# Two attentions: probabilities scaled before they are transposed, and the values matmul turned round

## What is computed

```
def masked_softmax(s, mask):
    s = jnp.where(mask, s.astype(jnp.float32), NEG)
    pr = jax.nn.softmax(s, axis=-1)
    return jnp.where(mask, pr, 0.0)
...
    gt = jax.nn.sigmoid(gates.astype(jnp.float32)).reshape(B, T, 3, NSA_HEADS, 1)
    out = (gt[:, :, 0] * to_bthd(o_cmp) + gt[:, :, 1] * to_bthd(o_sel)
           + gt[:, :, 2] * to_bthd(o_win))
```

```
        p = masked_softmax_2(jnp.concatenate([s_sel, s_own], axis=-1),
                           jnp.concatenate([m_sel, m_own], axis=-1)).astype(v.dtype)
...
        return (jnp.einsum('hqnk,hqnkd->hqd', p_sel, v_sel)
                + jnp.einsum('hqk,hqkd->hqd', p_own, v_own))
...
    mixed = jax.nn.sigmoid(ga) * (o_a @ w_proj_a) + jax.nn.sigmoid(gb) * (o_b @ w_proj_b)
```

## Time and profile before

| | before |
|---|---|
| median of 3 runs | 1384.17 us (1383.19 to 1384.9) |
| profiled execution | 1385.43 us, its span 1383.6 us |
| TensorE busy | 1177.2 us, 85% of the span |
| VectorE, ScalarE, GpSimd busy | 471.0, 255.0, 144.9 us |
| mean granted clock | 0.936 of full speed |
| read from memory | 328.64 MB |
| chain that ended last | DMA 22%, TensorE 16%, ScalarE 3%, VectorE 2% of the span |

### The profile page before, as it was taken

One profiled execution on the slowest core, in us unless ns is written; L12 is line 12 of the kernel. 1 busy time (PEld: TensorE's weight loads), 2 busy tenths in 40 slices (PEclk: granted clock), 3 DMA queues, 4 the chain that ended last, 5 costly groups with the idle time before them and its releaser, 6 DMA issues. The chain is left out here.

```text
span 1383.6 us, 14289 instructions
## 1 busy us (share of the span) xinstructions
PE 1177.2 (85%) x6103; PEld 672.5 (49%) x6103; DVE 471.0 (34%) x771; ACT 255.0 (18%) x502; POOL 144.9 (10%) x159
## 2 busy tenths in 40 slices
PE   7999999999999999999999999997656375564636
PEld 7946655555865999444544446453212031221312
DVE  7672333024715554644784452231001010010101
ACT  2331003125611212001222265011000000000001
POOL 1111004010110124431032000100000000000000
PEclk9999999999999999999999999999788787887879
DMA  9641223352115544344353210898999999999994
GB/s 385 243 182 62 90 95 120 112 211 103 62 37 207 191 183 164 140 182 165 140 196 135 81 59 31 359 412 336 427 429 427 428 427 429 428 429 428 428 423 175
DMA packets 27701, 330.68 MB, mean 239 GB/s; under 512 B 4192, under 2 KB 4976, under 8 KB 7408
## 3 DMA queue, kind: packets, MB, share of 16 engines
q1 hardware_dynamic: 27632, 329.70, 59.1%
HBM read 328.64 MB, written 1.05 MB: 238 GB/s over the span
## 5 line engine op out<-in xcount | busy, mean ns | idle before, releaser
L228 PE MATMUL ps<-ring,arena 128*128 128x512 f32 (+2 forms) x1880 | 685.5, 620 | 88.2 <-DMA ring<-in_w 49.1
L228 PE MATMUL ps<-arena 128*128 128x128 f32 (+9 forms) x2706 | 512.2, 420 | 78.5 <-DMA ring<-in_w 22.1
L228 PEld LDWEIGHTS ps<-ring,arena 128*128 128x128 f32 (+2 forms) x1880 | 261.1, 164 | 402.6 <-issue 396.8
L228 PEld LDWEIGHTS ps<-arena 128*128 128x128 f32 (+3 forms) x2706 | 290.2, 171 | 227.5 <-issue 190.7
L1944 DVE TENSOR_TENSOR arena<-ps,junk 128x512 f32<-128x512 f32 x8 | 5.5, 692 | 366.7 <-PE ps L228 366.7
L228 PE MATMUL ps<-misc,arena 128*32 128x512 f32 (+3 forms) x216 | 83.1, 546 | 23.2 <-DMA arena<-in_w 23.2
L228 PE MATMUL ps<-arena,ring 128*128 128x128 f32 x768 | 88.1, 275 | 0.0
L228 PEld LDWEIGHTS ps<-arena,ring 128*128 128x128 f32 x768 | 87.0, 192 | 0.5 <-issue 0.5
L231 PE MATMUL ps<-cst,arena 128*128 128x128 f32 x456 | 60.0, 275 | 5.2 <-ACT arena L474 2.1
L231 PEld LDWEIGHTS ps<-cst,arena 128*128 128x128 f32 x456 | 51.4, 141 | 26.6 <-issue 16.3
L367 DVE TENSOR_TENSOR arena<-ring 128x2048 f32<-128x2048 f32 (+1 forms) x19 | 36.8, 1937 | 40.4 <-PE ps L228 39.5
(11 more groups left out here) (275 smaller groups left out, 642.1 us busy)
## 6 DMA issues: line engine op xcount, KB each, us to landing
arena<-in_w SPq DMA_DIRECT2D x42, 2048.0 KB, 35.0
ring<-in_w SPq DMA_DIRECT2D x42, 2048.0 KB, 34.2
ring<-in_w_in SPq DMA_DIRECT2D x27, 2048.0 KB, 7.9
ring<-in_w_up SPq DMA_DIRECT2D x8, 2048.0 KB, 8.3
ring<-in_w_down SPq DMA_DIRECT2D x8, 2048.0 KB, 7.8
misc<-in_w SPq DMA_DIRECT2D x8, 2048.0 KB, 34.7
ring<-in_w_out SPq DMA_DIRECT2D x4, 2048.0 KB, 14.6
ring<-in_w_branch_a SPq DMA_DIRECT2D x2, 2048.0 KB, 10.1
```

The costliest lines, as they stand in the source:

```text
L228: return lambda q: q.matmul(out_, l, r, start=s, stop=e, skip_group_check=skip)
```

## The change

The reciprocal of the row sums (times the gate, in the first attention) is taken in a new step `normed`, and GpSimd multiplies the exponentials by it before they are transposed. `pipeline` writes it behind `soft` of the next job. In `values` the roles are exchanged: the values of a head (128 keys x 64) are stationary, the transposed probabilities move, and heads with even and odd place write to PSUM partitions 0-63 and 64-127, two column tiles. In the first attention two heads that share their values go through one matmul (`per_v` is 2), 256 columns; in the second each head has its own, 128 columns. The outputs come out with features on partitions. So in the first block the compressed branch is transposed into `YBT` ahead of the pipeline and each job adds its output there; in the second each job copies into `OT`. The transposes behind are gone, and in the second attention the copy of the transposed probabilities moves from ScalarE to VectorE.

```diff
+        def attention(m, heads, q_of, k_of, v_of, per_v, mask, PT, coef_of, finish, *tokens):
...
+            def normed():
+                t = dve.op(lambda q: q.reciprocal(cc, su), state["e"])
+                gate = coef_of(m, heads)
+                if gate is not None:
+                    t = dve.op(lambda q: q.tensor_tensor(cc, cc, gate, ALU.mult), t)
+                aux[("g", r3_)] = state["e"] = pool.op(lambda q: q.tensor_tensor(S3, S3, cc.unsqueeze(2).broadcast_to([128, H, nk]), ALU.mult), t)
+
             def turned():
...
-                t = act.op(lambda q: q.activation(PT[b], P[:, :], ACT.Copy), t, aux.get(("p", b)))
+                if coef_of(m, heads) is None:
+                    t = dve.op(lambda q: q.tensor_copy(PT[b], P[:, :]), t, aux.get(("p", b)))
+                else:
+                    t = act.op(lambda q: q.activation(PT[b], P[:, :], ACT.Copy), t, aux.get(("p", b)))
...
             def values():
                 P, i = unit()
+                pt = PT[b].rearrange("p (a k q) -> p a k q", a=H, k=m + 1)
                 fns = []
-                for a, h in enumerate(heads):
+                for a0 in range(0, H, 2 * per_v):
                     for kt in range(m + 1):
-                        x = (a * (m + 1) + kt) * 128
-                        fns.append(mm(P[:, a * 64:a * 64 + 64], PT[b][:, x:x + 128], v_of(h, kt), kt == 0, kt == m))
+                        for r in range(2):
+                            o = P[64 * r:64 * r + 64, a0 * 64:(a0 + 2 * per_v) * 64]
+                            fns.append(mm(o, v_of(heads[a0 + r], kt), pt[:, a0 + r:a0 + 2 * per_v:2, kt, :], kt == 0, kt == m))
...
@@ pipeline
                 if x < n:
                     jobs[x][3]()
+                if 1 <= x < n + 1:
+                    jobs[x - 1][4]()
                 if x % every == 0:
                     fill(1)
...
+        ybt = [turn_half(OBN, YBT, None, m, cmp_t[m], qt_toks) for m in range(2)]
+
+        def fin_nsa(m, heads, P, t):
+            c = heads[0] // 2
+            o = YBT[:, c:c + len(heads) // 2, m * 128:m * 128 + 128]
+            ybt[m] = dve.op(lambda q: q.tensor_tensor(o, P, o, ALU.add), t, ybt[m])
+            return ybt[m]
...
-        pipeline(jobs, 2, lambda: ybt.append(turn_half(OBN, YBT, None, 0, ob_tok[0], qt_toks)))
+        pipeline(jobs, 2)
...
-                a = dve.op(lambda q: q.tensor_tensor(OO[w][:, m, heads[0]:heads[0] + H], P[:, 0:H * 64].rearrange("p (h d) -> p h d", h=H),
-                                                     cc.unsqueeze(2).broadcast_to([128, H, 64]), ALU.mult), a)
...
+                a = dve.op(lambda q: q.tensor_copy(o, P), t)
...
-        pipeline(jobs, 1, lambda: turn_out(0))
+        pipeline(jobs, 1)
...
-        proj_a.pop(0)()
-        turn_out(1)
-        t_ot = [pe.now(), act.now()]
+        t_ot = [pe.now(), act.now(), dve.now(), pool.now()]
```

More of the change, by code:

```diff
@@ L1004, in build @@
         sm = sb("sm", 32)
+        cn4 = sb("cn4", 32)
         aux = {"s": 0}
-        def attention(m, heads, q_of, k_of, v_of, mask, PT, finish, *tokens):
+        def attention(m, heads, q_of, k_of, v_of, per_v, mask, PT, coef_of, finish, *tokens):
             H, nk = len(heads), 128 * (m + 1)
@@ L1013, in attention @@
             nm, su = nmx[:, r3_ * 8:r3_ * 8 + H], sm[:, r3_ * 8:r3_ * 8 + H]
+            cc = cn4[:, r3_ * 8:r3_ * 8 + H]
             state = {}
@@ L1051, in values @@
                 P, i = unit()
+                pt = PT[b].rearrange("p (a k q) -> p a k q", a=H, k=m + 1)
                 fns = []
-                for a, h in enumerate(heads):
+                for a0 in range(0, H, 2 * per_v):
                     for kt in range(m + 1):
-                        x = (a * (m + 1) + kt) * 128
-                        fns.append(mm(P[:, a * 64:a * 64 + 64], PT[b][:, x:x + 128], v_of(h, kt), kt == 0, kt == m))
+                        for r in range(2):
+                            o = P[64 * r:64 * r + 64, a0 * 64:(a0 + 2 * per_v) * 64]
+                            fns.append(mm(o, v_of(heads[a0 + r], kt), pt[:, a0 + r:a0 + 2 * per_v:2, kt, :], kt == 0, kt == m))
                 t = pe.group(fns, state["p"], unit_users[i])
                 aux[("p", b)] = t
-                unit_users[i] = aux[("g", r3_)] = finish(m, heads, P, su, t)
-            return scores, turned, values, soft
+                unit_users[i] = finish(m, heads, P[:, 0:H * 64].rearrange("p (c q) -> p c q", q=128), t)
+            return scores, turned, values, soft, normed
         def pipeline(jobs, every, late=None):
@@ L1140, in build, with gate_of @@
         tap("ocmp", U(11), cmp_t)
[L1142 to L1157, removed]
+        YBT = U(3).rearrange("p (c t) -> p c t", c=8)
+        OBN = U(11).rearrange("p (m n) -> p m n", m=2)
+        ybt = [turn_half(OBN, YBT, None, m, cmp_t[m], qt_toks) for m in range(2)]
[4 more added lines that the diff above has]
+            return ybt[m]
+        def gate_of(branch):
+            return lambda m, heads: gt3[:, m, branch * 16 + heads[0]:branch * 16 + heads[0] + len(heads)]
         def qr_of(h, m):
@@ L1170, in build @@
                         lambda h, nk, KTT=KTT: KTT[64 * (h % 2):64 * (h % 2) + 64, h // 4, 0:nk],
[L1171 to L1175, removed]
+                        lambda h, kt, voff=voff: KV[:, kt, voff + (h // 4) * 64:voff + (h // 4) * 64 + 64], 2,
+                        cmask[:, 128:256] if m == 0 else cmask[:, 0:256], PT1, gate_of(br), fin_nsa,
+                        qrt_toks, qt_toks, kd[kn], t_cm, kv_toks, cmp_t, t_gt))
         MTT = U(4).rearrange("p (c t) -> p c t", c=8)
@@ L1180, in build @@
         PTT = U(13)[:, 1024:1536].rearrange("p (c t) -> p c t", c=2)
[L1181 to L1183 removed]
+        mtt, t_v, t_h1, t_h2, t_u = [], [], [], [], []
+        pipeline(jobs, 2)
         while fillers:
@@ L1197, in build @@
         weigh_by_half(lambda i: A["w_branch_b"][i], YBT, 8, ybt, GB, gb_t, GA, mg_t,
-                      {(0, 0): lambda: ybt.append(turn_half(OBN, YBT, None, 1, ob_tok[1], qt_toks)), (0, 1): None, (1, 0): None,
+                      {(0, 0): None, (0, 1): None, (1, 0): None,
                        (1, 1): lambda: mtt.append(turn_half(GA, MTT, None, 0, mg_t[0]))})
@@ L1582, in build, with f @@
         SS[2] = U(12, 0.5)
-        OO = [U(6, 0.5).rearrange("p (m h d) -> p m h d", m=2, h=8), U(6, 0.5, 1024).rearrange("p (m h d) -> p m h d", m=2, h=8)]
+        OT = [U(7, 0.5).rearrange("p (c t) -> p c t", c=4), U(7, 0.5, 1024).rearrange("p (c t) -> p c t", c=4)]
         PT2 = [U(13, 0.5), U(13, 0.5, 1024)]
-        fin_toks = [[], []]
+        ot = [[], []]
         def fin2(w):
[L1589 to L1592, removed]
-                a = dve.op(lambda q: q.tensor_tensor(OO[w][:, m, heads[0]:heads[0] + H], P[:, 0:H * 64].rearrange("p (h d) -> p h d", h=H),
-                                                     cc.unsqueeze(2).broadcast_to([128, H, 64]), ALU.mult), a)
-                fin_toks[w].append(a)
+            def f(m, heads, P, t):
+                c = heads[0] // 2
+                o = OT[w][:, c:c + len(heads) // 2, m * 128:m * 128 + 128]
+                a = dve.op(lambda q: q.tensor_copy(o, P), t)
+                ot[w].append(a)
                 return a
@@ L1610, in build @@
                         lambda h, nk, kT=kT: kT[64 * (h % 2):64 * (h % 2) + 64, h // 2, 0:nk],
[L1611 to L1625, removed]
-        pipeline(jobs, 1, lambda: turn_out(0))
-        tap("o2", U(6), fin_toks)
+                        lambda h, kt, vv=vv: vv[:, kt, h * 64:h * 64 + 64], 1,
+                        mask, PT2, lambda m, heads: None, fin2(w), tT[qn], tT[kn], tV[vn], t_dm if w else t_cm, pe.now()))
+        pipeline(jobs, 1)
         fill(8)
```

## The result

The changed kernel takes **1392.02 us** (median of 5 runs, 1391.46 to 1392.9) against 1384.17 us: ratio 1.0053, 95% interval 1.0042 to 1.0065, so slower. Its profiled execution took 1391.66 us, span 1389.9 us; that of before 1385.43, span 1383.6.

What follows compares the result with a forecast made beforehand. TensorE's own sequence was taken to bound the kernel up to about 932 us. First attention +10.6 and second -2.0 gave +8.6 us, so a median of 1392.8, range 1387 to 1403.

Steps and rivals of the forecast that it cites:

- first scores to the projection behind transposes(0): Start of the first attention: the first transposes wait 5.64 us less one scores group, +4.6 us.
- three pairs with a projection: First attention, projections in every second iteration: 14.67 us, then 15.74 twice, from one to the next; +1.9, +1.2, +1.2.
- three iterations without one: First attention, three iterations without a projection: 13.07 us instead of 11.46, +1.6.
- tail: End of the first attention, from transposes(9) on: 9.8 us instead of 9.69, +0.1.
- second attention with its transposes: Second attention: shorter values and absent output transposes save 6.1 us, waits at start and end cost 4.1; -2.0 us.
- Values at 1.07: Both attentions: a values group in two column tiles takes 1.07 us instead of 1.82, bounds 0.86 and 1.82.
- rival 2: Column tiles give nothing and values stay at 1.82 us: +7.1, 1399.9 us; chance 0.08.
- The handoff of 5.64: From the end of the next job's scores to a job's transposes: 5.64 us, 2.37 of it the GpSimd multiply.
- The clock: First attention stage: if new gaps bring the granted clock to the lower level, the time lies above the forecast; no size.
- Weights: Behind the second attention: early expert weights issued some 5 us sooner, counted as nothing.
- Rival 1: TensorE's work alone decides, scaled tiles always ready in both attentions: 1368.2 us; chance 0.08 for any gain.
- Rival 3: GpSimd is held up beside VectorE, +1.31 us in 8.5 places: +11.1, 1403.9 us; chance 0.10.

Runs made afterwards that it cites:

- on_vector: The changed kernel with the multiply by the reciprocals on VectorE instead of GpSimd: 1388.99 us, ratio 1.003 to the kernel before.
- second_only: Only the second attention is changed, the first stays as in the kernel before: 1382.12 us, ratio 0.9987.
- no_scaling: The changed kernel without reciprocal, gate and GpSimd multiply, so its output is wrong and only the attentions are read: 1412.33 us, not comparable.
- one_deeper: The changed kernel with one more pipeline iteration between scores and transposes: 1377.17 us, ratio 0.9948 to the kernel before.
- deeper_apart: The changed kernel with one more pipeline iteration and the first attention's projections in iterations 2, 5, 8 and 11: 1369.76 us, ratio 0.9899 to before.
- first_only: Only the first attention is changed, the second stays as in the kernel before: 1394.1 us, ratio 1.0075.
- tiles_apart: The changed kernel issuing all values matmuls of one column tile, then all of the other: 1392.41 us, ratio 1.0074 to the kernel before.
- multiply_twice: The changed kernel with a second GpSimd multiply, by ones, ahead of the scaling one: 1418.63 us, ratio 1.026 to the kernel before.

## Why the prediction came out right, and where its steps were off

It forecast 1392.8 and the reason: slower, because the scaled tiles come late. Part by part, from the rows above:

| step | forecast | measured |
|---|---|---|
| transposes ahead of the pipeline | +0.9 | +0.9 |
| first scores to the projection behind transposes(0) | +4.6 | +4.6 (15.61 for 11.04), 0.4 of it clock |
| three pairs with a projection | +1.9, +1.2, +1.2 | +2.4 (1.25 clock), +0.4, +0.6 |
| three iterations without one | +1.6 | +0.95 |
| tail | +0.1 | -0.5 |
| group of transposes gone behind | -0.9 | -0.8 |
| second attention with its transposes | -2.0 | -1.8, 1.0 of clock in it |
| sum | +8.6 | +6.7 |

(The spans of the two traced executions differ by 6.3 us, and the one of the changed kernel is 0.6 us ahead at 310 us: 6.9 in all, 0.2 of it behind the second attention. The medians differ by 7.9.)

1. **What bounds it**: held. From the projection behind the second attention on, the rest is 521.4 us against 522.0 - 0.9 (the old output transposes), so the shift reaches the end.
2. **Values at 1.07**: held (1.07 and 1.08), and rival 2, no gain from column tiles, is out. The Trainium skill's page TensorEngine Tiling (Array Packing), section Key Properties, says that different tiles can load and multiply in parallel; the trace agrees, 1.08 with two tiles against 1.94 with one.
3. **The handoff of 5.64**: the place was right, the size was not. The multiply took 1.90, the lower bound, not the 2.37 that I took from the line through 256 and 512 elements, and the handoffs a little less than 0.1 each: 4.99 in all. In some 7 places that is 4.6 us too much. With a multiply of 1.90 the prediction's own sum, over its 8.5 places, would have been 8.6 - 4.0 = 4.6 and its median 1388.8, 3.2 us below the measured one. The page GPSIMD Engine Reference of the Trainium skill (section Elementwise — side-by-side cycle accounting), whose rate of about 2.6 cycles an element gave 2.2 us as an estimate, was nearer than my line, and still above the 1.90 measured.
4. **The clock**: named as what would make it wrong, but not in the sum. Against the same work elsewhere, 1.7 us behind the first wait (transposes 1.36 to the next start for 0.92, projection 8.22 for 6.97) and 1.0 at the end of the second attention (865.08 to 868.54, 3.46, where on_vector at full clock has 2.42, from 865.04 to 867.46). So 2.7 us of the 6.7 are clock, and they hid more than half of the error of point 3. The nearness of 1392.8 to 1392.02 is partly luck. on_vector's rows:

```profile
865.04 1.09 PE L228 MATMUL ps<-arena 128*64 128x128 f32 x16
866.43 1.09 PE L228 MATMUL ps<-arena 128*64 128x128 f32 x16 [0.29 <-DVE arena L1058]
```

5. **Second attention**: turn(0) came 0.1 later, not 0.7; the wait near the end was 2.35, not 3.05, both mostly by the shorter multiply (0.47 of 0.6 and of 0.7). That it gains at all is confirmed by second_only barely (interval to 0.9999), and there not by the stage in the trace.
6. **Weights**: issued some 2.4 us behind the start of the last values instead of 7.5, and worth nothing, as counted (without the old transposes the rest grew by 0.2).
7. **Rival 1**, TensorE's work alone: needs the chain hidden. no_scaling and one_deeper show that it does come then, but not in full: ScalarE's exponentials and copies leave 3.0 us of waits in either. With the projections apart as well, deeper_apart takes 1369.76 us, 1.6 above the 1368.2 of that rival. **Rival 3**, GpSimd held up, is out: 1892 to 1897 ns.

What is shown: the scaling costs 13.8 us in the first attention, against a gain of 5.4 for the rest of the change there, and 12.2 us go away when the transposes stand one iteration further off. What is only argued: the split of the measured +6.7 into multiply and clock, which rests on one trace. first_only has the same first attention and took 3.3 us longer in it, though its waits for GpSimd are less (14.0 us against 15.1), so the clock's part differs by some 4 us from one execution to another.

## What to carry to other kernels

A step added between two engines costs its whole length only where the pipeline has no work beside it: compare the sum of the chain, with what stands ahead of each link in its engine's queue, with the other engine's work in that time. If it is longer, lengthen the distance or put large work into the gap before touching the step; here one iteration and another place for four projections turned +8 us into -14, with the same instructions. And a wait on TensorE costs more than itself if the clock falls behind it.

## What the runs showed of the hardware

- The granted clock fell to the 1.2 GHz level behind short stops of TensorE, and not each time behind the same one. first_only, at the very place where after kept 1.00 (transposes in 1.09 us at 359.48 behind 1.77 us):

```profile
355.26 1.97 PE L231 MATMUL ps<-cst,arena 128*128 128x128 f32 x8 [1.77 <-POOL arena L1050]
```

```profile
356.00:358.00 2.00, 2.00 (x8) 1.48 (x7) 0.33 (x3) 0.73 (x1) 1.56 (x1) 0.50 0.00 0
```

- It also falls with TensorE busy throughout, in some executions only. The same stretch ahead of the change, behind 32 records of 48 columns (16 matmuls), in before, with the window 250 to 300 us:

```profile
251.30 3.67 PE L228 MATMUL ps<-misc,arena 128*128 128x48 f32 x32
254.90 15.87 PE L228 MATMUL ps<-ring,arena 128*60 128x256 f32 x80
```

```profile
250.00:300.00 50.00, 50.00 (x217) 29.23 (x216) 6.94 (x20) 9.68 (x15) 4.72 (x14) 0.90 0.42 171
```

And in tiles_apart:

```profile
255.29 14.19 PE L228 MATMUL ps<-ring,arena 128*60 128x256 f32 x80
```

```profile
250.00:300.00 50.00, 50.00 (x232) 29.00 (x231) 6.94 (x20) 10.76 (x17) 4.72 (x14) 1.00 0.43 175
```

Seven of the 14 traced executions had 0.90 there, and their first attention begins at 313.6 to 315.0 us; six had 1.00 and begin at 310.2 to 311.2 (multiply_twice had 0.97, 311.3). That is some 4 us, half of what was to be measured here. The code of this stretch is the same in all. In the low case the engine lost time twice, in the rows above and, further on, in 48 records of 64 columns and the projection behind them (6.47 and 9.03 us in before, 5.44 and 7.11 in tiles_apart).

- GpSimd multiplied 1024 elements by a value repeated over 128 or 256 of them in 1.89 us, 1.85 ns an element, while the additions of L1155 took 2.85 and 2.50 ns an element.
